# A two-layer decoder step: the second mixer in one block with the first layer's experts, its projections split up among the turns of its attention

## What is computed

```
def trunk(x, ...):
    for li in range(2):
        if li == 0:  tok, mq, state = mixer_a(x, ...)              # chunkwise mLSTM, 6 heads x 128
        else:
            k, v = split(x @ w_kv_shared)                          # two key maps, 6 heads x 64 each; values 6 x 128
            q12, mq = split(x @ w_in_b)                            # two query maps, and the memory queries
            tok = mixer_b(q12, k, v, past pages for the samples)   # softmax(q1 k1) - lam * softmax(q2 k2), times v
        m = mem_attention(mq, mem_k[li], mem_v[li])                # 4 heads x 64, 256 memory tokens
        x = layer_norm(ALPHA * x + concat(tok, m) @ w_out[li])
        x = layer_norm(ALPHA * x + hier_moe(x))                    # 16 experts, two for each token
```

## Time and profile before

| | |
|---|---|
| median of 3 timed runs | 1430.04 us (1427.33 to 1432.54) |
| the profiled execution's own time | 1434.98 us |
| its span, first to last instruction | 1433.1 us |
| mean granted TensorE clock | 0.893 |
| busy: TensorE / VectorE / ScalarE | 1175.5 / 416.5 / 251.7 us |
| HBM read and written | 307.6 and 47.3 MB, 248 GB/s over the span |
| experts of layer 0 and 1 | about 441 to 599 and 1212 to 1382 us |
| mixer B with its memory attention | 651 to 1095 us |

### The profile page before, as it was taken

One profiled execution on the slowest core, in us unless ns is written; L12 is line 12 of the kernel. 1 busy time (PEld: TensorE's weight loads), 2 busy tenths in 40 slices (PEclk: granted clock), 3 DMA queues, 4 the chain that ended last, 5 costly groups with the idle time before them and its releaser, 6 DMA issues. The chain is left out here.

```text
span 1433.1 us, 22516 instructions
## 1 busy us (share of the span) xinstructions
PE 1175.5 (82%) x9072; PEld 706.3 (49%) x9072; DVE 416.5 (29%) x1055; ACT 251.7 (18%) x659; POOL 58.1 (4%) x76
## 2 busy tenths in 40 slices
PE   6999999779877999618899997777868962999950
PEld 5888888645452333217677774333444421333310
DVE  2222223244331111182000022334543431111118
ACT  2112222030111111031000021222451010111111
POOL 4000000000020000020000000000000002000011
PEclk9999999879987999958999999998567985999985
DMA  9973332268256999375999939997034424899943
GB/s 343 371 208 96 90 99 66 78 258 352 94 206 232 387 423 425 125 240 176 333 391 384 381 121 354 404 363 300 1 117 159 193 118 178 305 420 426 423 168 140
DMA packets 124455, 356.42 MB, mean 249 GB/s; under 512 B 10287, under 2 KB 57568, under 8 KB 113214
## 3 DMA queue, kind: packets, MB, share of 16 engines
q1 hardware_dynamic: 106046, 291.65, 54.7%
q0 software_dynamic: 9344, 34.92, 6.3%
q10 hardware_dynamic: 8960, 28.40, 5.1%
HBM read 307.59 MB, written 47.33 MB: 248 GB/s over the span
## 5 line engine op out<-in xcount | busy, mean ns | idle before, releaser
L1300 PE MATMUL bank<-W,XT 128*32 128x512 f32 x1728 | 195.0, 604 | 2.4 <-DVE XT L1379 2.4
L1300 PEld LDWEIGHTS bank<-W,XT 128*32 128x32 f32 x1728 | 53.8, 111 | 124.2 <-issue 120.5
L1061 PE MATMUL bank<-WOUT,CAT 128*128 128x512 f32 x256 | 111.6, 594 | 0.0
L1929 PE MATMUL bank<-XT,W 128*128 128x260 f32 x448 | 107.1, 396 | 0.0
L471 PE MATMUL bank<-XT,WH 128*128 128x260 f32 x448 | 100.0, 384 | 0.0
L1322 PE MATMUL bank<-WD,GT 128*32 128x512 f32 x864 | 98.2, 595 | 1.6 <-DVE GT L1400 1.6
L1929 PEld LDWEIGHTS bank<-XT,W 128*128 128x128 f32 x448 | 85.5, 195 | 17.0 <-issue 4.3
L471 PEld LDWEIGHTS bank<-XT,WH 128*128 128x128 f32 x448 | 84.5, 190 | 13.3
L471 PE MATMUL bank<-WH,XT 128*128 128x256 f32 x384 | 84.0, 379 | 0.0
L471 PEld LDWEIGHTS bank<-WH,XT 128*128 128x128 f32 x384 | 72.5, 190 | 10.0 <-issue 0.4
L1061 PEld LDWEIGHTS bank<-WOUT,CAT 128*128 128x128 f32 x256 | 48.0, 190 | 57.9 <-issue 57.8
(11 more groups left out here) (382 smaller groups left out, 1308.0 us busy)
## 6 DMA issues: line engine op xcount, KB each, us to landing
W<-in_w13f SPq DMA_DIRECT2D x38, 2048.0 KB, 15.0
PGS<-in_KP SPq DMA_DIRECT2D x128, 384.0 KB, 5.8
PGS<-in_VP SPq DMA_DIRECT2D x128, 384.0 KB, 5.6
WD<-in_w2f SPq DMA_DIRECT2D x38, 1024.0 KB, 12.2
CAT<-XS ACTq DMA_DIRECT2D x27, 512.0 KB, 9.2
WH<-in_w_a SPq DMA_DIRECT2D x13, 1024.0 KB, 12.0
XS<-CAT POOLq DMA_DIRECT2D x20, 512.0 KB, 16.0
WOUT<-in_w_out SPq DMA_DIRECT2D x4, 2048.0 KB, 12.4
```

Of the source, the lines that this page charges most:

```text
L1061: last = nc.tensor.matmul(PB[2 * (i % 2) + c][:, :], CAT[:, k, t * P:(t + 1) * P], w_out(c)[:, k, :], start=(k == 0), stop=(k == KC - 1))
L1300: last = nc.tensor.matmul(PB[2 + g % 2][32 * j:32 * j + 32, :], XGT[:, g % 2, k, 32 * j:32 * j + 32], W13[:, LANES[g][j] % WRING, k, :], s ...
L1929: last = nc.tensor.matmul(bank_of(u)[0:u["m"], 0:u["w"]], u["lhsT"](w, k), u["rhs"](w, k), start=(k == 0), stop=(k == KC - 1))
```

## The change

1. **One block.** `experts`, `extra_tiles` and `combine` return functions for each engine instead of making blocks. For layer 0 they stand in the same block as mixer B, in front of its own items on every queue; for layer 1 in one block of their own. In place of the barriers: `y_all`, which ScalarE counts up behind the last stored expert rows, and on which GpSimd's gathers and SyncE's loads wait. The four half slabs 4, 0, 1, 2 go out during the last expert groups, `WV` (three value slabs) behind the norm's weights.
2. **The norm behind the experts** (`combination`). The second sum pass gives its row sum as well (`accum_out`); ScalarE squares the row with the mean as bias and sums it, then Sqrt; VectorE's two last passes stay. bn_stats and bn_aggr go. The order is `residual(i + 1)` before `normed(i)`. The transposes use two banks in one turn (`turns=1`).
3. **Projections.** The sample rows' queries are projected by three units on 8 rows right behind the norm of the sample tile, turned, and put into `QD`; with three value units these are the first seven. Then three value units a tile (`items` of kind `tile`) between the transposes of the tiles, with the first 8 K groups among them. Slabs of K and Q are cut so that one slab holds a pair of heads of both maps (`half_slab`, runs of 128 columns), so that 8 units are enough for heads 0 and 1, and 20 units follow among the turns: two in each of turns 0 to 5, one in each of turns 6, 8, 10, 12 and 18 to 21. They all use bank 3; the scores of odd turns share bank 2.
4. **Places.** `PGS` moves to the front of the ring, over `YG` and `GB` of the norm: the load of group 0 waits for the third tile's norm, of group 1 for the fourth, of groups 2 and 3 for the fifth. The turns go by pairs of heads, (3, 0, 3, 0, 2, 1, 2, 1) with heads alternating. The prompt's heads are kept in `Q12` in place of `XT`.
5. **Others.** The new K and V are stored behind the last unit as before, which now stands in turn 21. The output weights use `WOUT0`, asked for behind the last page and memory pieces; in layer 1, W13 of experts 1 and 2 comes behind the output projection instead of W2 of experts 0 to 3. `WG` is the first load on SyncE's queue instead of ScalarE's.

By the planner, the order is now: 12 `tile` items with K groups 0 to 7, 8 units with K groups 8 to 21, then turns. K groups end in front of unit 31 (turn 2), `own` stands at units 35 and 36, `pt` from unit 37, V groups start in front of the values of turn 6 and end in front of turn 20, the memory pieces stand in turn 22 to `post` 4.

```diff
-        W2 = at("W2", 0, [P, 4, KC, 256])
+        W2 = at("W2", 49152, [P, 4, KC, 256])
...
+            def on_act(act, behind=None):
...
+                def deviation(i):
+                    t, n = ORDER[i], n0 + i
+                    r = rows(t)
+                    st = LNS[0:r, n % 2, :]
+                    act.wait_ge(var_ready, n + 1)
+                    act_chain.link(act, nc.scalar.activation(YG[0:r, t, 0, :], X[0:r, t, :], ACT.Square, bias=st[:, 2:3], accum_out=st[:, 3:4]))
+                    nc.scalar.activation(st[:, 14:15], st[:, 3:4], ACT.Sqrt, scale=1.0 / D, bias=st[:, 16:17]).then_inc(sd_ready, 1)
...
+                for i, t in enumerate(ORDER):
+                    if i + 3 < NT:
+                        weigh(i + 3)
+                    if behind:
+                        transposed_out(nc, act, t, n0 + i, 1)
+                    if i + 2 < NT:
+                        deviation(i + 2)
+                    if behind:
+                        behind(i)
...
+                    dve_chain.link(dve, stt(x, x, ALPHA, y0, ALU.mult, ALU.add))
+                    stt(x, y1, WT2[0:r, 1, t:t + 1], x, ALU.mult, ALU.add, accum_out=st[:, 0:1]).then_inc(sum_done, 1)
+                    dve.wait_ge(sum_done, NT * l + i + 1)
+                    nc.vector.tensor_scalar(st[:, 2:3], st[:, 0:1], -1.0 / D, None, ALU.mult).then_inc(var_ready, 1)
...
+                    dve_chain.link(dve, nc.vector.reciprocal(st[:, 15:16], st[:, 14:15]))
+                    dve_chain.link(dve, stt(x, x, st[:, 2:3], GB[0:r, 0, :], ALU.add, ALU.mult))
+                    stt(x, x, st[:, 15:16], GB[0:r, 1, :], ALU.mult, ALU.add).then_inc(xn_ready, 1)
...
-        items = [("unit", i) for i in range(nu)]
-        for n in range(len(turns)):
-            items += [("weights", n), ("values", n)]
+        items = [("tile", i) for i in range(V0, U0)] + [("unit", i) for i in range(U0, EARLY)]
+        late = {n: 2 for n in range(6)}
+        late.update({n: 1 for n in (6, 8, 10, 12, 18, 19, 20, 21)})
+        at_unit = EARLY
+        for n in range(len(turns)):
+            items.append(("weights", n))
+            for step in ("values", None):
+                if (step is None) < late.get(n, 0):
+                    items.append(("unit", at_unit))
+                    at_unit += 1
+                if step:
+                    items.append(("values", n))
...
+                experts0["sp"](sp)
+                for n in range(4):
+                    if n % 2 == 0:
+                        sp.wait_ge(h_done, LAST[13 + n // 2] + 1)
+                    sp.dma_start(half_place((0, 4, 1, 2)[n], n), half_slab((0, 4, 1, 2)[n])).then_inc(half_in[n], 16)
+                extra0["sp"](sp)
+                combine0["sp"](sp)
+                for c in range(3):
+                    sp.dma_start(WV[:, c, :, :], half_slab(7 + c)).then_inc(wv_in[c], 16)
...
                     if n >= 4:
                         sp.wait_ge(*place_free(n - 4))
+                    else:
+                        sp.wait_ge(xn_ready, combine0["first"] + (3, 4, 5, 5)[n])
...
+                for i in range(V0):
+                    unit(i)
+                    if i == 4:
+                        transpose_tile(nc, pe, ORDER[1], n0 + 1, 1)
+                for k in range(U0 - V0):
+                    samples(k)
+                    t, c = divmod(k, 3)
+                    if c == 0:
+                        pe.wait_ge(xt_out, n0 + t + 2)
+                    if c == 2 and t + 2 < NT:
+                        transpose_tile(nc, pe, ORDER[t + 2], n0 + t + 2, 1)
+                    unit(V0 + k)
```

More of the change, by code:

```diff
@@ L929, in build @@
         half_in = [sem(f"half_in{i}") for i in range(4)]
+        wv_in = [sem(f"wv_in{c}") for c in range(3)]
         kv_out = sem("kv_out")
@@ new lines, in on_pe, with body @@
+            def on_pe(pe):
+                def body(k, n):
+                    pe.wait_ge(ov_x, (n + 1) * 16)
+                    for c in range(KC):
+                        last = nc.tensor.transpose(PB[c // 4][:, (c % 4) * P:(c % 4 + 1) * P], XG[:, 0, c * P:(c + 1) * P], ident)
+                    last.then_inc(ov_t, 1)
+                    pe.wait_ge(ov_tc, (n + 1) * 2)
+                    pe.wait_ge(ov_w1, (n + 1) * 16)
+                    for c in range(KC):
+                        last = nc.tensor.matmul(PB[2][0:OVR, :], XOT[:, c, :], W13[:, 0, c, :], start=(c == 0), stop=(c == KC - 1))
+                    last.then_inc(ov_h, 1)
+                    pe.wait_ge(ov_g, n + 1)
+                    for c in range(2):
+                        last = nc.tensor.transpose(PB[4][:, c * P:(c + 1) * P], GA[:, 0, c * P:(c + 1) * P], ident)
+                    last.then_inc(ov_gt, 1)
+                    pe.wait_ge(ov_gc, n + 1)
+                    pe.wait_ge(ov_w2, (n + 1) * 16)
+                    for c in range(2):
+                        for q in range(2):
+                            last = nc.tensor.matmul(PB[5 + c][0:OVR, :], GOT[:, q, :], WD2[:, 0, q, c * 512:(c + 1) * 512],
+                                                    start=(q == 0), stop=(q == 1))
+                    last.then_inc(ov_y, 1)
+                count, done = number(pe)
+                pe.wait_ge(y_out, 2 * (BG + NG))
+                tiles(pe, count, done, body)
@@ L1668, in build @@
         before, now, at_piece, last_at = [], 0.0, 0, 0.0
-        landing = [8.0, 12.0, 16.0, 20.0]
+        landing = [9.0, 13.5, 18.0, 22.0]
         for kind, n in items:
             mine = []
-            while at_piece < len(pieces) and not (kind == "unit" and n < H + 1):
+            while at_piece < len(pieces):
                 piece = pieces[at_piece]
-                if piece[0] == "vown" and kind == "unit":
+                if kind == "tile" and pieces.index(piece) >= 4 * PAGES // 4:
+                    break
+                if piece[0] == "own" and items.index(("unit", K_ALL - 1)) + 2 > len(before):
+                    break
+                if piece[0] == "cms" and items.index(("unit", nu - 1)) + 2 > len(before):
                     break
@@ L1700, in build @@
             if kind == "unit":
-                plan += [("half", w + 4) for w in range(6) if after[w] == n]
-            if kind == "values" and n == len(turns) - 1:
-                plan.append(("out", 0))
+                plan += [("half", n)] if n in follows else []
+        plan.append(("out", 0))
         lam_in, lam_sum, lam_exp, qd_ready, vnew_ready = (sem(n) for n in ("lam_in", "lam_sum", "lam_exp", "qd_ready", "vnew_ready"))
@@ L1784, in piece_k @@
                         if f == 0:
-                            pe.wait_ge(qd_ready, 1)
+                            pe.wait_ge(proj_dve, units[TURNED]["emptied"])
                         if f >= 2:
@@ L1959, in _ @@
                 for k, (kind, n) in enumerate(items):
+                    if kind == "tile":
+                        continue
                     samples(k)
@@ L2073, in mem_exponentials, with values_out @@
                     last.then_inc(ms_exp, 1)
+                def values_out(i):
+                    for n in range(V0) if i == 0 else range(V0 + 3 * i - 3, V0 + 3 * i):
+                        unit(n)
+                experts0["act"](act)
+                extra0["act"](act)
+                combine0["act"](act, values_out)
                 act.wait_ge(lam_sum, 1)
@@ L2300, in build, with _ @@
         output_and_norm(1)
-        feed_forward(1, lambda sp: None, O["y"])
+        experts1, extra1, combine1 = feed_forward(1)
+        with nc.Block() as block:
+            @block.sync
+            def _(sp):
+                experts1["sp"](sp)
+                extra1["sp"](sp)
+                combine1["sp"](sp)
+                for i, t in enumerate(ORDER):
+                    sp.wait_ge(xn_ready, combine1["first"] + i + 1)
+                    store(sp, O["y"][t * P:t * P + rows(t), :], X[0:rows(t), t, :])
+                sp.wait_ge(out_done, 16 * stores[0])
+            @block.gpsimd
+            def _(pool):
+                combine1["pool"](pool)
+            @block.tensor
+            def _(pe):
+                experts1["pe"](pe)
+                extra1["pe"](pe)
+            @block.scalar
+            def _(act):
+                experts1["act"](act)
+                extra1["act"](act)
+                combine1["act"](act)
+            @block.vector
+            def _(dve):
+                experts1["dve"](dve)
+                extra1["dve"](dve)
+                combine1["dve"](dve)
 OUTS = {
```

693 lines of the change are left out of this document (353 added, 340 removed).

## The result

| | before | after |
|---|---|---|
| median of the timed runs | 1429.7 us (1424.8 to 1437.8, 8 runs) | 1418.6 us (1414.7 to 1426.7, 8 runs) |
| ratio after / before, 95% interval | | 0.9927 (0.9897 to 0.9956) |
| profiled execution: time, span | 1434.98, 1433.1 us | 1417.93, 1416.1 us |

The change makes the kernel 11 us (0.7%) faster. I had forecast 42.5 us, with a range that ended at 1413. The profiled execution of before lay 5 us above its median, so the two traces differ by 17 us, 6 more than the medians do. Of the 17, 8 lie behind the start of the output projection (the norm) and 9 ahead of it, where I had forecast 34.

The account below looks back on a forecast made before the run. It took VectorE's norm to bound the end, and TensorE, the DMA stream or neither to be full by stretch before it. Mixer 34 plus norm 8.5 gave 42.5 us, so 1387.5 from 1430.0, range 1373 to 1400, widened to 1363 to 1413.

Parts of the forecast that it names:

- Joint of the layers: From layer 0's last store: first prompt tile's value unit starts at 641, against a first projection at 651.25.
- Tile stage: Value units and transposes of the prompt tiles, with eight K pages among them: ends at 706.
- Rest of K: K pages 12 to 31: stream needs 94 us, to 803; TensorE's own work is 86, so the stream decides.
- Ahead of V: From last K page to first V page, units, turns and new waits: V starts at 862, against 855 before.
- V pages: Stretch of the V pages: 46.2 MB in 125 us, to 987, against 133 before; TensorE's load of 119 barely fits.
- Tail: Behind the last V page: 74 us, so the second mixer ends at 1061 instead of 1095, gain 34.
- Norm: Behind layer 1's experts: 5.4 us a tile instead of 6.84, five times, and 1.8 from fewer barriers; gain 8.5.
- Gates' weights: Loaded first on SyncE's queue: TensorE could start some 3 us sooner; taken as 0, bounds -1 and +3.
- Slabs: K and Q slabs in runs of 512 bytes instead of 1 KB: taken as nothing, bounds nothing and 8 us.
- Rival B: Page stream is the bound, moved and not shortened: V stretch 133, tail 85, mixer ends 1080, total 1409; chance 0.16.
- C: Slower: every unit between turns waits on in-order queues and one bank; at 2.6 us each more, 1440; chance 0.08.
- signs of it being wrong: Bank or turn-weight waits over 25 us, page waits under 15, low tile-stage clock, or pages 2 and 3 well behind 670.

Follow-up runs that it names:

- the two runs with the light issue: SyncE reads page numbers without the bounds check, once in the changed kernel (ratio 0.9816) and once in the kernel before (0.9916).
- posts_ahead: Changed kernel in which VectorE scales all six heads' tokens before the sample tokens' memory pieces, instead of one head at each post; 1414.9 us, ratio 0.9899.
- slabs_one_run: Changed kernel with the ten half slabs in one array, a partition's part being one run of 8 KB; 1420.4 us, ratio 0.9890.
- sync_light: Changed kernel in which SyncE reads a page's number without the check of its bounds; 1403.1 us, ratio 0.9816.
- four_edits_and_slabs: Changed kernel with unchecked page numbers, score copies between value units, posts' scaling early, gates' weights on ScalarE's queue, and half slabs in 8 KB runs; 1383.7 us, ratio 0.9667.
- gate_weights_back: Changed kernel with the gates' weights on ScalarE's queue again instead of SyncE's, as in the kernel before; one run, 1414.25 us.

## Why the prediction was wrong, by its own steps

1. *Joint of the layers*: right as a sum (641.1 against 641), not in its parts. The barriers gave almost nothing: from the last store to the first gather it is 5.7 us instead of 6.0, since the wait for the store to land is what counts (5.4). The first weighing began 14.4 us behind the last store instead of 11.8 (615.07 and 600.63 against 611.41 and 599.60): the gathers are 2.6 us late, where I had 1.5. The estimate by the rule of the Trainium skill (DMA: Bandwidth & Descriptors, Queues, rings and completion order) was 6, which the trace does not bear out; no run takes the slabs away from the gathers.
2. *Tile stage*: right, 709 against 706.
3. *Rest of K*: **the first step that failed**: the last K page was used 14 us late, 3 of them from step 2. I had 94 us for the stream against 86 for TensorE, and 109 were measured. Without a stream it is still 99, so the term that was mis-sized most is TensorE's 86. It counted the scores of two turns, and scores that belong to five stand there (8.0 us, 20 of 96 matmuls); it left out ScalarE's copy of a full score bank (2.1), the waits for turns' weights (4.2, the first turn's alone 3.7) and the time stretched by the clock behind such stops. The stream's term was too small as well: twenty groups and the slabs took from 713.65 to 813.3, 100 us. That last group lay there for 3 us before TensorE came to it. When two bounds are 8 us apart, an error in the lower decides which one holds.
4. *Ahead of V*: 55 us against 59. Right in size, and shown to be TensorE's list: five kernels with this list whose last K page came at 809 to 818 began V at 869 to 873.
5. *V pages*: 130 against 125. The rate was mis-sized. The 371 GB/s of the earlier trace rows was pages and stores together; the pages alone were issued at 366 at most, in both kernels, which the two runs with the light issue show. Moving the stores behind the stream saved 4 us (134 to 130) and not the 8 that I had, since they had run beside the pages.
6. *Tail*: 83 against 74. The sample's memory pieces now fall between the posts, and VectorE's queue has them in front of each scaling. Posts and heads took 54 us where I had 46: TensorE's waits at the posts are 5 us longer than before (7.5 against 2.3), and posts_ahead takes 4 of them away. Some 4 more are this execution's clock, since two kernels with the same posts took 50. I had counted 46 because it was 46 before, when those pieces lay in front.
7. *Norm*: right, 8.0 against 8.5. Of its parts the norm gave 6.0 and not 7.2, the barriers and loads 2.0. The sum's output is a second instruction of 0.08 us, where my bound from ScalarE's read was 0.20. By the Trainium skill (VectorE: DVE Perf Modes, Two Vector instructions with no wait between them) an op that writes out its accumulator is two instructions, and the trace agrees; at 0.08 us it costs 0.4 for five tiles and not the 1.0 of the estimate.
8. *Gates' weights*: 0 against some 3 us lost at layer 0's output projection, at the upper bound that I gave. In the two traces 1.0 of them is left at the last store of layer 0's experts (600.63 against 599.60), and step 1 has it in its 641.1.
9. *Slabs*: 0, and right: slabs_one_run moves the same 348 GB/s over the K stretch in the same time.

Together 14 + 5 + 9 - 4 = 24, nearly all of the 25 us by which the mixer's 34 fell short in the trace. It is a sum over single traces, in which a stretch scatters by up to 4 us. The other 6 us of the error are the difference between the two profiled executions and the medians; they are no error of the mechanism. Rival B came nearest: V stretch, tail and end of the mixer (130, 83, 1086 against 133, 85, 1080) were nearly its own, but in part for another reason: B let the stream decide the K stretch too, where TensorE's list did. That its 1409 lay 10 us off and the forecast 31 is partly luck. C did not happen: the waits for turn weights stayed at 11.8 us and those for the one bank under 1. What I gave as signs of it being wrong did not show either, since none of them watched TensorE's own list.

## What to carry to other kernels

A busy share of 0.99 on the DMA engines does not say that they are the limit (359 GB/s at 0.99 here, and 388 at 1.01 with lighter issues): look at the spacing of the issues. If it is constant to the hundredth while slots have long been free, the issuing queue's own steps are the bound, and its register loads and checks are the first thing to thin out. Before a stage's time is forecast as the larger of two sums, price it with one of the two taken away, and give the smaller sum the same care. Work moved between two stages must be priced with what will then stand in front of it in each in-order queue, and units that cover a turn's latency are worth most where no pages are left. Before a shorter stretch is put down to an edit, look whether the same stretch has that length in some kernel without the edit: half of what posts_ahead seemed to give was the clock.

## What the runs showed of the hardware

- SyncE: a load of one number from SBUF takes 0.27 us, and with its bounds check the next step starts 0.56 us later (four of them and four issues: 4.30 us); without the check the same eight steps take 3.27 us. An issue with an address from a register takes 0.52 us from one to the next.
- The page stream with rows of 3 KB reached 388 GB/s at a share of 1.01 when it was issued every 3.79 us on average (sync_light, 871 to 990), and 359 at a share of 0.99 with the checked numbers (changed kernel, 890 to 990).
- A page issue behind a 1 MB slab in runs of 512 bytes held SyncE's queue for up to 3.05 us in the changed kernel and 7.88 in sync_light, instead of 0.33; behind a slab in runs of 8 KB for at most 1.33 (slabs_one_run) and 1.18 (four_edits_and_slabs). No total shows a cost of it.
- The same stretch of posts and memory heads, with the same waits, took 54.4 us at a granted clock of 0.72 and 50.3 at 0.83 (changed kernel and gate_weights_back, one execution each).
- VectorE's read of its accumulator (L1552) takes 0.08 us, against ScalarE's 0.20:
```profile
L1552 DVE DVE_READ_ACCUMULATOR X<-YG,WT,X x10: 71/83/84, 618.8 to 1407.4; 128x1 f32 x8, 8x1 f32 x2
```
